# Expert loop of a mixture-of-experts step: moving the two activation transposes from TensorE and ScalarE to VectorE, with weight rows loaded in a matching order

## Chip, core and metric

The kernel runs on one core of a Trainium2 chip. The metric is the device time of one execution in microseconds (us): the median of several runs. The profile is of one further execution.

## What is computed

The reference is one layer of a hybrid decoder (512 prompt tokens behind 16 learned meta tokens, and 8 sample tokens): a mixer (gated linear attention beside sliding-window attention), then a mixture of experts, then a final norm. Only the mixture of experts is touched. Cut to what matters:

```python
logits = x2d @ w_router + b_router              # 520 tokens, 32 experts
top_v, top_e = lax.top_k(logits, 4)
gates = softmax(top_v)
def expert_block(xb, e):                        # rows of one expert
    hh = xb @ w_up[e] + b_up[e]                 # 1024 -> 2048
    gate = minimum(hh[:, :1024], 7.0)
    lin = clip(hh[:, 1024:], -7.0, 7.0)
    a = gate * sigmoid(1.702 * gate) * (lin + 1)
    return a @ w_down[e] + b_down[e]            # 1024 -> 1024
y[token] += gates * expert_block(...)           # for the 4 chosen experts
```

Everything is float32. With the inputs that the reference draws, 2080 token slots fall on 32 experts. In blocks of at most 64 slots the experts 0 to 31 need 2 1 2 1 2 1 1 1 2 1 1 2 2 2 2 2 1 1 1 2 2 1 1 1 2 1 2 1 1 1 2 1 blocks, 46 in all: 14 experts take two blocks, 18 take one.

## The kernel before

The kernel first runs the mixer and the router and builds, on the chip, a table of blocks (which expert, which slots, and whether the block's expert is new). Then comes the expert loop, one pass per block of 64 slots, and at the end the four slot outputs of each token are summed and normalised.

**Weights.** `raw` holds the weights of one expert and no more: 12 units of 1 MiB, 8 of `w_up` (`load_up`, line 473) and 4 of `w_down` (`load_down`, line 561). A unit gives each of 128 partitions 8 KiB: one row of `w_up` (2048 numbers) or two rows of `w_down` (2 x 1024). Up unit j is the rows 128j to 128j+127, down unit j the rows 256j to 256j+255, so each unit is one stretch of memory. SyncE asks for them. It refills a unit as soon as TensorE has used it in this block (`up_used`, `dn_used`), and only if the next block has a new expert. So the weights of a new expert stream in while the last block of the old one is computed, and no earlier.

**Rows.** GpSimd gathers the 64 tokens of a block with an indirect DMA (`gather`, line 443). The 128 partitions of `x_rows` hold 64 slots twice: partitions 0 to 63 the first 512 features of each, partitions 64 to 127 the last 512. The same halves hold the up projection in PSUM (banks 0 and 1), the activations `act_g`, and the output `y_rows`, which GpSimd scatters to memory (`scatter`, line 451). GpSimd waits for a scatter to land before it issues the next gather (line 467).

**Transposes before.** The matmuls need features on partitions. `turn_x` (line 1608) transposes the gathered rows on TensorE in four 128x128 pieces into PSUM bank 3, and `move_xT` (line 780) copies them to `xT` on ScalarE. `turn_a` (line 1614) and `move_aT` (line 784) do the same for the activations through PSUM bank 4 into `aT`.

**Order of the work.** Each engine's order is written out by hand. In loop pass b TensorE does `up(b)` (line 1628), `turn_x(b + 1)`, `down(b - 1)` (line 1647), `turn_a(b)`: the down projection is one block behind, so that the activation function (`clamp`, line 1220, `swiglu`, line 1225, on VectorE and `sigmoid` on ScalarE) runs beside it. `up` makes 32 matmul calls over 8 units, `down` 16 over 4 units; each call is two records in the profile, and the two 64-column halves of the array run side by side. After the first unit of `up(b)` TensorE runs `find(b + 1)` (line 1601), a small product that lists the tokens of the next block. ScalarE does `sigmoid(b)`, `move_xT(b + 1)`, `y_out(b - 1)`, `move_aT(b)`. VectorE does, in this order: `indices(b + 1)`, `select` for the up bias, `find_slots(b + 2)`, `clamp(b)`, `swiglu(b)`, `pick_outputs(b - 1)`, `select` for the down bias. GpSimd does `gather(b + 1)`, `scatter(b - 1)`. SyncE does 8 up loads for block b and 4 down loads for block b - 1.

Of the kernel before, what the change touches and what calls it, by code (L numbers as in the profile page):

```python
# [63 lines left out]
def moe_layer(nc, x_prompt, x_sample, state_gla, cache_k, cache_v, meta, bias_tab, g_mix, w_in, w_a_up, b_a,  # L64
# [12 lines left out]
    with ExitStack() as ctx:  # L77
        def sem(name):
            return ctx.enter_context(nc.semaphore(name))
# [51 lines left out]
        xT = R("xT", [P, 4, P])  # L131
        aT = R("aT", [P, 4, P])
# [168 lines left out]
        xT_psum, xT_ready = sem("xT_psum"), sem("xT_ready")  # L301
# [3 lines left out]
        aT_psum, aT_ready = sem("aT_psum"), sem("aT_ready")  # L305
# [70 lines left out]
        def _(pool):  # L376
# [66 lines left out]
            def gather(b):  # L443
                pool.wait_ge(idx_ready, b + 1)
                if not (isinstance(b, int) and b == 0):
                    pool.wait_ge(xT_psum, b)
                pool.sem_inc(rows_asked, 1)
                pool.indirect_dma_start(x_rows[:], None, xn_halves,  # L448
                                        bass.IndirectOffsetOnAxis(ap=row_idx[:, 0:1], axis=0),
                                        bounds_check=last_row, oob_is_err=False).then_inc(gathered, 16)  # L450
# [21 lines left out]
        def _(sp):  # L472
            def load_up(e, j, cond):
                src = w_up[0, column(e), P * j:P * j + P, :].rearrange("a p n -> p (a n)")
# [86 lines left out]
            def load_down(e, j, cond):  # L561
                src = w_down[0, column(e), 2 * P * j:2 * P * (j + 1), :].rearrange("a (p r) n -> p (a r n)", r=2)
# [47 lines left out]
        def _(act):  # L610
# [169 lines left out]
            def move_xT(b):  # L780
                act.wait_ge(xT_psum, b + 1)
                act.activation(xT[:], ps[:, 3, :].rearrange("p (k q) -> p k q", k=4), ACT.Copy).then_inc(xT_ready, 1)  # L782

            def move_aT(b):
                act.wait_ge(aT_psum, b + 1)
                act.activation(aT[:], ps[:, 4, :].rearrange("p (k q) -> p k q", k=4), ACT.Copy).then_inc(aT_ready, 1)

# [10 lines left out]
            move_xT(0)  # L798
            sigmoid(0)
            move_xT(1)  # L800
            move_aT(0)
            act.wait_ge(table_made, 1)
            nb = block_count(act)
            with act.Fori(1, nb) as b:
                sigmoid(b)
                move_xT(b + 1)
                y_out(b - 1)
                move_aT(b)
# [8 lines left out]
        def _(dve):  # L817
# [412 lines left out]

            find_slots(own, 0)
            indices(own, 0)
            select(sel_up, 0, sel_up_ready)
            find_slots(own, 1)
            indices(own, 1)
# [6 lines left out]
            swiglu(own, 0)  # L1242
            before_loop = own.n
            nb = block_count(dve)
            with dve.Fori(1, nb) as b:
# [7 lines left out]
                swiglu(o, b)  # L1253
                pick_outputs(b - 1)
                dve.wait_ge(dn_bias_done, b)
                select(sel_dn, b, sel_dn_ready)
                assert o.n == STEPS, o.n
# [32 lines left out]
        def _(pe):  # L1290
# [317 lines left out]
            def turn_x(b):  # L1608
                pe.wait_ge(gathered, 16 * b + 16)
                for h in range(4):  # L1610
                    ins = pe.transpose(ps[:, 3, P * h:P * h + P], x_rows[:, P * h:P * h + P], ident[:])  # L1611
                ins.then_inc(xT_psum, 1)

            def turn_a(b):

                pe.wait_ge(a_ready, b + 1)
                for h in range(4):
                    u, r = h // 2, h % 2
                    ins = pe.transpose(ps[:, 4, P * h:P * h + P], act_g[:, 2 * P * u + r:2 * P * (u + 1):2], ident[:])  # L1619
                ins.then_inc(aT_psum, 1)  # L1620

# [6 lines left out]
            def up(b):  # L1628
# [6 lines left out]
                pe.wait_ge(xT_ready, b + 1)  # L1635
                for j in range(UPU):
                    pe.wait_ge(landed[j], 16 * b + 16)
                    for bank in range(2):
                        for i in range(2):
                            c = FF * bank + HF * i  # L1640
                            ins = mm(ps[SUB * i:SUB * i + SUB, bank, :], xT[:, j % 4, SUB * (j // 4):SUB * (j // 4) + SUB],  # L1641
# [5 lines left out]
            def down(b):  # L1647
# [3 lines left out]
                pe.wait_ge(aT_ready, b + 1)  # L1651
                for j in range(DNU):
                    pe.wait_ge(landed[UPU + j], 16 * b + 16)
                    for r in range(2):
                        for i in range(2):
                            ins = mm(ps[SUB * i:SUB * i + SUB, 2, :], aT[:, 2 * (j % 2) + r, SUB * (j // 2):SUB * (j // 2) + SUB],  # L1656
# [6 lines left out]
            turn_x(0)  # L1663
            up(0)
            turn_x(1)
            turn_a(0)
# [50 lines left out]
```

## Time and profile before

| | us |
|---|---|
| Median of 3 runs | 1549.63 (1547.12 to 1549.8) |
| The profiled execution, its own time | 1542.3 |
| Its span, first to last instruction | 1540.5 |
| Expert loop, from the second block's index list to the last down matmul (382.55 to 1489.87) | 1107.3 |

The page gives the engines' busy time over the span: TensorE matmuls 1393.8 us (90%), VectorE 412.1 us (27%), ScalarE 217.8 us (14%), GpSimd 108.2 us (7%). How to read it: the span falls into the mixer and router (to about 347 us), the loop, and the final sum (from about 1490 us), and the loop itself is not even, since a block whose successor has the same expert asks for no weights. The expert loop has to be read by stretches between such blocks, with the memory rate of each beside it.

### The profile page before, as it was taken

Reading aid. Unit: us, or ns where it says so; the run is one execution under the profiler, and the core shown is the slowest. Engines: PE = TensorE matmul, PEld = TensorE weight load, DVE = VectorE, ACT = ScalarE, POOL = GpSimd, SP = SyncE. Lnnn points to the kernel's source line nnn. Section 1 sums busy time; section 2 is a strip of 40 time slices with the busy share of each in tenths; the row PEclk is TensorE's granted clock in tenths of the full one; section 3 lists DMA queues with packets and bytes.
Section 4 is the critical chain, followed back from the end, with each engine's and each line's share of the span. In section 5 each row is a group of like instructions: output and inputs, shape, how many; then the busy total and the mean of one; then the engine's idle time right before and its main releaser. Section 6 shows DMA issues by size and latency. Waiting matters only on the chain.

```text
span 1540.5 us, 21414 instructions
## 1 busy us (share of the span) xinstructions
PE 1393.8 (90%) x6999; PEld 580.4 (38%) x6999; DVE 412.1 (27%) x1011; ACT 217.8 (14%) x419; POOL 108.2 (7%) x151
## 2 busy tenths in 40 slices
PE   8999999966999999899999999998999899998960
PEld 7866556632333333233333333332333233332310
DVE  3433356632211211121112112211111112211118
ACT  4121233310001010000101001000000001000002
POOL 3000000000010000001010010000001010000100
PEclk9989969987999999999999999999999999999985
DMA  9313101253989899999966678999699998999856
GB/s 356 77 47 123 50 16 56 110 204 128 394 340 378 346 398 421 421 402 422 401 253 242 253 330 336 397 422 420 241 413 421 421 398 353 399 422 421 372 202 266
DMA packets 83515, 464.98 MB, mean 302 GB/s; under 512 B 11890, under 2 KB 20708, under 8 KB 33074
## 3 DMA queue, kind: packets, MB, share of 16 engines
q1 hardware_dynamic: 75438, 445.69, 71.8%
q0 software_dynamic: 7440, 17.30, 3.0%
q10 hardware_dynamic: 612, 1.67, 0.3%
q8 instruction: 15, 0.25, 0.1%
q14 instruction: 10, 0.08, 0.0%
HBM read 625.47 MB, written 22.38 MB: 421 GB/s over the span
## 4 chain that ended last, share of the span: by engine, by line
PE 58%; DMA 30%; DVE 4%; issue 4%; ACT 2%; SPq 1%; POOLq 0%; DVEq 0%
PE ps L1656 18%; PE ps L1641 17%; DMA x_rows<-expert_inputs,row_idx 11%; DMA slot_outputs<-y_rows,out_idx 11%; DMA raw<-in_w_down_dram 8%; PE ps L1354 4%; PE ps L1331 4%; PE ps L1553 4%; PE ps L1611 2%; PE ps L1624 2%; DVE t_x L1283 1%; ACT y_rows L795 1%; PE ps L1619 1%; PE ps L1514 1%; PE ps L1513 1%
## 5 line engine op out<-in xcount | busy, mean ns | idle before, releaser
L1641 PE MATMUL ps<-raw,xT 128*64 128x512 f32 x2944 | 656.3, 596 | 14.4 <-DMA raw<-in_w_up_dram 14.4
L1641 PEld LDWEIGHTS ps<-raw,xT 128*64 128x64 f32 x2944 | 205.1, 137 | 399.5 <-issue 355.6
L1656 PE MATMUL ps<-raw,aT 128*64 128x512 f32 x1472 | 328.1, 595 | 8.4 <-DMA raw<-in_w_down_dram 8.1
L1656 PEld LDWEIGHTS ps<-raw,aT 128*64 128x64 f32 x1472 | 102.4, 137 | 203.6 <-issue 178.3
L1222 DVE TENSOR_SCALAR act_g<-ps 128x512 f32<-128x512 f32 x46 | 31.8, 691 | 447.9 <-PE ps L1641 447.9
L790 ACT ACTIVATE act_s<-act_g 128x512 f32<-128x512 f32 x46 | 29.0, 630 | 700.9 <-DVE act_g L1222 700.9
L1207 DVE TENSOR_REDUCE found<-ps 128x2 f32<-128x8 f32 x47 | 7.8, 166 | 411.3 <-PE ps L1604 411.3
L456 POOL DMA_INDIRECT slot_outputs<-y_rows,out_idx x46 | 46.3, 1007 | 750.5 <-ACT y_rows L795 750.5
L795 ACT ACTIVATE y_rows<-ps 128x512 f32<-128x512 f32 x46 | 27.5, 598 | 303.4 <-PE ps L1656 303.4
L448 POOL DMA_INDIRECT x_rows<-expert_inputs,row_idx x47 | 48.6, 1034 | 299.5 <-issue 265.3
L1611 PE MATMUL ps<-ident,x_rows 128*128 128x128 f32 x188 | 31.6, 291 | 37.2 <-DMA x_rows<-expert_inputs,row_idx 37.2
L1354 PE MATMUL ps<-w_c_cols,hT 128*128 128x512 f32 x128 | 59.4, 618 | 0.0
L1553 PE MATMUL ps<-w_out_sb,mixT 128*128 128x512 f32 x128 | 56.7, 597 | 2.5 <-DVE mixT L1056 2.5
L1611 PEld LDWEIGHTS ps<-ident,x_rows 128*128 128x128 f32 x188 | 20.1, 142 | 76.1 <-DMA x_rows<-expert_inputs,row_idx 59.9
L1619 PEld LDWEIGHTS ps<-ident,act_g 128*128 128x128 f32 x184 | 25.4, 207 | 39.0 <-issue 36.5
L1199 DVE TENSOR_TENSOR hit<-slots_row,shifted 128x640 bf16<-128x640 f32 x48 | 39.6, 825 | 1.6
L1331 PE MATMUL ps<-hT,w_a_cols 128*128 128x268 f32 x160 | 36.6, 390 | 0.0
L1619 PE MATMUL ps<-ident,act_g 128*128 128x128 f32 x184 | 34.2, 308 | 2.3 <-DVE act_g L1229 2.3
L1354 PEld LDWEIGHTS ps<-w_c_cols,hT 128*128 128x128 f32 x128 | 24.6, 197 | 29.7 <-issue 29.7
L1553 PEld LDWEIGHTS ps<-w_out_sb,mixT 128*128 128x128 f32 x128 | 23.7, 190 | 30.9 <-issue 30.6
L1331 PEld LDWEIGHTS ps<-hT,w_a_cols 128*128 128x128 f32 x160 | 30.3, 190 | 6.1 <-issue 0.4
L782 ACT ACTIVATE xT<-ps 128x512 f32<-128x512 f32 x47 | 27.6, 588 | 32.8 <-PE ps L1611 32.7
(309 smaller groups left out, 918.6 us busy)
## 6 DMA issues: line engine op xcount, KB each, us to landing
raw<-in_w_up_dram SPq DMA_DIRECT2D x368, 1024.0 KB
raw<-in_w_down_dram SPq DMA_DIRECT2D x184, 1024.0 KB
t_slots<-slot_outputs SPq DMA_DIRECT2D x8, 1024.0 KB, 13.4
w_c_cols<-in_w_in_dram SPq DMA_DIRECT2D x1, 4096.0 KB, 31.2
w_out_sb<-in_w_out_dram SPq DMA_DIRECT2D x1, 4096.0 KB, 14.7
w_a_cols<-in_w_in_dram SPq DMA_DIRECT2D x1, 2624.0 KB, 13.0
x_sb<-in_x_prompt_dram SPq DMA_DIRECT2D x4, 512.0 KB, 5.5
w_b_cols<-in_w_in_dram SPq DMA_DIRECT2D x1, 2048.0 KB, 17.9
```

The lines of the kernel that those rows point to most:

```text
L448: pool.indirect_dma_start(x_rows[:], None, xn_halves, bass.IndirectOffsetOnAxis(ap=row_idx[:, 0:1], axis=0), bounds_check=last_row, oob_is ...
L456: pool.indirect_dma_start(slot_halves, bass.IndirectOffsetOnAxis(ap=out_idx[:, 0:1], axis=0), y_rows[:], None, bounds_check=last_out, oob_ ...
L795: act.activation(y_rows[:], ps[:, 2, :], ACT.Copy).then_inc(y_ready, 1)
L1199: dve.tensor_tensor(hit[:], slots_row[:, 0:SUB].unsqueeze(1).unsqueeze(1).to_broadcast(everywhere), shifted[:].unsqueeze(2).unsqueeze(2).t ...
L1222: dve.tensor_scalar(act_g[:], ps[:, 0, :], LIMIT, None, ALU.min).then_inc(g_ready, 1)
L1331: ins = mm(ps[:, n % 4, 0:HALF], w[:, k, c0:c0 + P], hT[:, k, half], start=(k == 0), stop=(k == KT - 1))
L1354: ins = mm(ps[:, bank, 0:n], hT[:, k, a:z], w[:, k, c0:c0 + n], start=(k == 0), stop=(k == KT - 1))
L1553: ins = mm(ps[0:r, 6 + n, :], mixT[:, k, 0:r], w_out_sb[:, k, 512 * n:512 * n + 512], start=(k == 0), stop=(k == KT - 1))
L1611: ins = pe.transpose(ps[:, 3, P * h:P * h + P], x_rows[:, P * h:P * h + P], ident[:])
L1619: ins = pe.transpose(ps[:, 4, P * h:P * h + P], act_g[:, 2 * P * u + r:2 * P * (u + 1):2], ident[:])
L1641: ins = mm(ps[SUB * i:SUB * i + SUB, bank, :], xT[:, j % 4, SUB * (j // 4):SUB * (j // 4) + SUB], raw[:, SLOT[j], c:c + HF], start=False, ...
L1656: ins = mm(ps[SUB * i:SUB * i + SUB, 2, :], aT[:, 2 * (j % 2) + r, SUB * (j // 2):SUB * (j // 2) + SUB], raw[:, SLOT[UPU + j], D * r + HF ...
```

## The change

The two TensorE transposes, their PSUM banks and the two ScalarE copies are taken out. VectorE transposes from SBUF to SBUF in 32x32 squares: 8 instructions for a block's rows and 8 for its activations, each reading 32 partitions x 256 numbers with a stride and writing 32 partitions x 256 numbers. A square transpose can move a group of 32 features only as a whole, so feature 8p + c now lies on partition p in slice c. The weight rows must stand in the same order: up unit c is now the rows c, 8 + c, 16 + c, ... (8 KiB on each partition as before, 64 KiB apart in memory), down unit c the row pairs 8p + 2c, 8p + 2c + 1 (8 KiB, 32 KiB apart). In VectorE's order `turn_x(b + 1)` comes right after `swiglu(b)`, and `turn_a(b)` last in the pass. `turn_a(b)` waits until `down(b - 1)` has read the old `aT`; `turn_x(b + 1)` waits until `up(b)` is done with `xT` and the gather has landed. `gather(b)` now waits for VectorE's transposes of block b - 1.

```diff
-        xT = R("xT", [P, 4, P])
-        aT = R("aT", [P, 4, P])
+        xT = R("xT", [P, UPU, SUB])
+        aT = R("aT", [P, DNU, 2, SUB])
...
             def gather(b):
                 pool.wait_ge(idx_ready, b + 1)
                 if not (isinstance(b, int) and b == 0):
-                    pool.wait_ge(xT_psum, b)
+                    pool.wait_ge(xT_ready, 8 * b)
...
             def load_up(e, j, cond):
-                src = w_up[0, column(e), P * j:P * j + P, :].rearrange("a p n -> p (a n)")
+                src = w_up[0, column(e)].rearrange("a (p c) n -> c p (a n)", c=UPU)[j]
...
             def load_down(e, j, cond):
-                src = w_down[0, column(e), 2 * P * j:2 * P * (j + 1), :].rearrange("a (p r) n -> p (a r n)", r=2)
+                src = w_down[0, column(e)].rearrange("a (p c r) n -> c p (a r n)", c=DNU, r=2)[j]
...
             with act.Fori(1, nb) as b:
                 sigmoid(b)
-                move_xT(b + 1)
                 y_out(b - 1)
-                move_aT(b)
...
+            def turn(dst, dst_at, src, src_at, done):
+                for side in range(2):
+                    for group in range(2):
+                        rows_in = slice(SUB * side + 32 * group, SUB * side + 32 * group + 32)
+                        for parity in range(2):
+                            rows_out = slice(SUB * side + 32 * parity, SUB * side + 32 * parity + 32)
+                            dve.transpose(dst_at(dst[rows_out], group), src_at(src[rows_in], parity)).then_inc(done, 1)
+            def turn_x(b):
+                if not (isinstance(b, int) and b == 0):
+                    dve.wait_ge(up_used, UPU * b)
+                dve.wait_ge(gathered, 16 * b + 16)
+                turn(xT, lambda t, group: t[:, :, 32 * group:32 * group + 32],
+                     x_rows, lambda t, parity: t.rearrange("p (q r c) -> p q c r", q=2, c=UPU)[:, parity], xT_ready)
+            def turn_a(b):
+                dve.wait_ge(a_ready, b + 1)
+                dve.wait_ge(dn_used, DNU * b + 2 * DNU)
+                turn(aT, lambda t, group: t[:, :, :, 32 * group:32 * group + 32],
+                     act_g, lambda t, parity: t.rearrange("p (q r c t) -> p q c t r", q=2, c=DNU, t=2)[:, parity], aT_ready)
...
                 clamp(b)
                 swiglu(o, b)
+                turn_x(b + 1)
                 pick_outputs(b - 1)
                 dve.wait_ge(dn_bias_done, b)
                 select(sel_dn, b, sel_dn_ready)
+                turn_a(b)
...
                 bias(1, FF, sel_up).then_inc(up_bias_done, 1)
-                pe.wait_ge(xT_ready, b + 1)
+                pe.wait_ge(xT_ready, 8 * b + 8)
...
             with pe.Fori(1, nb) as b:
                 up(b)
-                turn_x(b + 1)
                 down(b - 1)
-                turn_a(b)
```

The slices of `xT` and `aT` that `up` and `down` read change to match. Ahead of the loop `turn_x(0)` stands after `find_slots(1)`, and `turn_x(1)` and `turn_a(0)` after `swiglu(0)`.

## Rows read from the trace of the kernel before

**Rows 1.** The page: memory rate in 40 equal slices of the span.

```profile
GB/s 356 77 47 123 50 16 56 110 204 128 394 340 378 346 398 421 421 402 422 401 253 242 253 330 336 397 422 420 241 413 421 421 398 353 399 422 421 372 202 266
```

**Rows 2.** Timeline of one pass without a wait (start us, us, engine, line, tile).

```profile
926.18 0.14 PEld L1641 LDWEIGHTS ps<-raw,xT 128*64 128x64 f32 x2 [0.28 <-issue]
927.14 0.66 PE L1611 MATMUL ps<-ident,x_rows 128*128 128x128 f32 x4
...
927.73 0.41 PE L1624 MATMUL ps<-bias_parts,sel_dn 128*64 128x512 bf16 x2
...
927.97 7.03 PE L1656 MATMUL ps<-raw,aT 128*64 128x512 f32 x32
...
934.93 0.74 PE L1619 MATMUL ps<-ident,act_g 128*128 128x128 f32 x4
...
935.60 0.62 PE L1624 MATMUL ps<-bias_parts,sel_up 128*64 128x512 bf16 x4
...
938.08 12.24 PE L1641 MATMUL ps<-raw,xT 128*64 128x512 f32 x56
```

**Rows 3.** The same timeline and its next pass: VectorE, GpSimd, and TensorE behind a gather.

```profile
927.26 0.69 DVE L1222 TENSOR_SCALAR act_g<-ps 128x512 f32<-128x512 f32 x1 [9.40 <-PE ps L1641]
...
927.86 0.68 DVE L1223 TENSOR_SCALAR act_l<-ps 128x512 f32<-128x512 f32 x1
...
929.31 0.69 DVE L1229 TENSOR_TENSOR act_g<-act_l,act_s 128x512 f32<-128x512 f32 x1
...
944.37 1.02 POOL L448 DMA_INDIRECT x_rows<-expert_inputs,row_idx  x1 [6.87 <-issue]
...
951.51 0.66 PE L1611 MATMUL ps<-ident,x_rows 128*128 128x128 f32 x4 [1.19 <-DMA x_rows<-expert_inputs,row_idx]
```

**Rows 4.** Waits between 382.55 and 1489.87 us (total us, times, longest).

```profile
PE ps L1611 <- DMA x_rows<-expert_inputs,row_idx: 28.1, 23, 2.1
...
PE ps L1641 <- DMA raw<-in_w_up_dram: 14.4, 21, 1.3
```

**Rows 5.** Windows cut at starts of L1207: length, busy time (PE, PEld, DVE, ACT, POOL), PEclk, DMA share, GB/s.

```profile
382.55:451.89 69.34, 69.34 (x347) 24.21 (x345) 14.18 (x40) 6.93 (x12) 6.09 (x6) 1.00 0.87 353
451.89:524.99 73.10, 71.05 (x347) 24.59 (x345) 14.27 (x39) 7.04 (x12) 6.44 (x6) 0.98 0.88 360
524.99:652.13 127.14, 117.55 (x577) 39.69 (x575) 23.73 (x65) 11.88 (x20) 10.15 (x10) 1.00 1.01 413
652.13:748.29 96.16, 92.67 (x462) 32.28 (x460) 18.91 (x53) 9.57 (x16) 8.12 (x8) 1.00 0.99 406
748.29:938.29 190.00, 185.19 (x922) 64.56 (x920) 37.89 (x105) 18.93 (x32) 16.29 (x16) 1.00 0.69 281
...
1064.40:1111.51 47.11, 46.29 (x232) 16.14 (x230) 9.46 (x26) 4.73 (x8) 4.06 (x4) 1.00 0.69 273
...
1237.54:1307.97 70.43, 69.42 (x347) 24.22 (x345) 14.20 (x40) 7.04 (x12) 6.09 (x6) 1.00 0.91 371
1307.97:1434.28 126.31, 117.54 (x577) 39.68 (x575) 23.63 (x65) 11.89 (x20) 10.15 (x10) 1.00 1.00 414
1434.28:1489.87 55.59, 51.84 (x247) 17.14 (x243) 9.61 (x27) 4.73 (x8) 4.06 (x4) 1.00 0.67 268
```

**Rows 6.** Groups by line, 400 to 1450 us: a short VectorE instruction (busy us, mean ns).

```profile
L1217 DVE TENSOR_TENSOR sel_up<-expert_of_row,blk_expert 128x64 bf16<-128x64 f32 x43 | 9.7, 225 | 5.3
```

**Rows 7.** Timeline of the loop's start: first rows landed, first block's end.

```profile
357.71 1.11 PE L1611 MATMUL ps<-ident,x_rows 128*128 128x128 f32 x4 [9.04 <-DMA x_rows<-expert_inputs,row_idx]
...
359.61 3.62 PE L1641 MATMUL ps<-raw,xT 128*64 128x512 f32 x8
...
377.94 0.69 DVE L1229 TENSOR_TENSOR act_g<-act_l,act_s 128x512 f32<-128x512 f32 x1
...
380.29 1.91 PE L1641 MATMUL ps<-raw,xT 128*64 128x512 f32 x8
```

**Rows 8.** Window 1506 to 1518 us, while `t_slots` loads 8 KiB pieces 16 KiB apart (columns as rows 5).

```profile
1506.00:1518.00 12.00, 0.00 (x0) 0.00 (x0) 10.65 (x10) 4.17 (x7) 0.00 (x0) 0.50 1.01 427
```

More of the change, by code:

```diff
@@ L300, in moe_layer @@
         out_idx_ready, y_free = sem("out_idx_ready"), sem("y_free")
-        xT_psum, xT_ready = sem("xT_psum"), sem("xT_ready")
+        xT_ready = sem("xT_ready")
         sel_up_ready, sel_dn_ready, up_bias_done, dn_bias_done = (
@@ L304, in moe_layer @@
         g_ready, up_read, sigm_ready, a_ready = sem("g_ready"), sem("up_read"), sem("sigm_ready"), sem("a_ready")
-        aT_psum, aT_ready = sem("aT_psum"), sem("aT_ready")
+        aT_ready = sem("aT_ready")
         y_ready, scattered = sem("y_ready"), sem("scattered")
@@ L778, in _ @@
             act.wait_ge(mixer_left, 4)
[L780 to L786, printed above, removed]
             def sigmoid(b):
@@ L797, in _ @@
             act.sem_inc(y_ready, 1)
-            move_xT(0)
             sigmoid(0)
-            move_xT(1)
-            move_aT(0)
             act.wait_ge(table_made, 1)
@@ L1234, in _ @@
             find_slots(own, 1)
+            turn_x(0)
             indices(own, 1)
@@ L1242, in _ @@
             swiglu(own, 0)
+            turn_x(1)
+            turn_a(0)
             before_loop = own.n
@@ L1606, in find @@
                 ins.then_inc(list_psum, 1)
[L1608 to L1620, printed above, removed]
             def bias(bank, c0, sel):
@@ L1640, in up @@
                             c = FF * bank + HF * i
-                            ins = mm(ps[SUB * i:SUB * i + SUB, bank, :], xT[:, j % 4, SUB * (j // 4):SUB * (j // 4) + SUB],
+                            ins = mm(ps[SUB * i:SUB * i + SUB, bank, :], xT[:, j, :],
                                      raw[:, SLOT[j], c:c + HF], start=False, stop=(j == UPU - 1))
@@ L1650, in down @@
                 bias(2, 2 * FF, sel_dn).then_inc(dn_bias_done, 1)
-                pe.wait_ge(aT_ready, b + 1)
+                pe.wait_ge(aT_ready, 8 * b + 8)
                 for j in range(DNU):
@@ L1655, in down @@
                         for i in range(2):
-                            ins = mm(ps[SUB * i:SUB * i + SUB, 2, :], aT[:, 2 * (j % 2) + r, SUB * (j // 2):SUB * (j // 2) + SUB],
+                            ins = mm(ps[SUB * i:SUB * i + SUB, 2, :], aT[:, j, r, :],
                                      raw[:, SLOT[UPU + j], D * r + HF * i:D * r + HF * i + HF], start=False,
@@ L1662, in _ @@
             find(0)
-            turn_x(0)
             up(0)
-            turn_x(1)
-            turn_a(0)
             pe.wait_ge(table_made, 1)
```

## Prediction

> **What bounds the kernel now.** I read the page first: its row of memory rates [rows 1] sits at 421 to 422 GB/s in some slices of the loop and at 241 to 253 in others. So one share of busy time cannot answer; the loop has to be cut where the need for weights changes. A block whose successor has the same expert asks for nothing; all others ask for 12 MiB. I therefore cut the loop at the start of the last block of each two-block expert, and took a window for each stretch up to the next such cut [rows 5]. Counting the experts between cuts by the list of blocks, there are four kinds: **pairs** (2 blocks, 1 weight load; five of them, four standing together in the window of 190.00 us), **triples** (3 blocks, 2 loads; three), one **quad** (4 blocks, 3 loads), and **quintets** (5 blocks, 4 loads; four, of which the first and the last are shown, 127.14 and 126.31). A tail of 55.59 us holds the last two blocks, and the first block stands ahead of the first cut.
>
> Pairs run at 273 to 281 GB/s: memory has room, TensorE decides. Quintets run at 413 to 414 GB/s with a DMA share of 1.00, and 5 blocks take 126.3 us, 25.3 each: memory decides. Next I read TensorE's side in one pass without waits [rows 2]: transposes at 927.14, down bias, down, transposes at 934.93, up bias, up with the small list product inside, and the next transposes at 950.25 would close a pass of 23.1 us. Three such passes are 69.3, exactly the first triple [rows 5]. The rest of a pair is one wait: GpSimd may gather only when its last scatter has landed, so the rows come about 1.2 us after TensorE wants them [rows 3], 28.1 us over 23 passes [rows 4].
>
> **TensorE's part of the change.** `turn_x` occupies 927.14 to 927.73, 0.59 us; `turn_a` 934.93 to 935.60, 0.67 us [rows 2]. Both go: 1.26 us a pass, so a pass is 23.11 - 1.26 = 21.85 us. Bounds: the gap in weight loads around a transposing step, 926.18 to 927.73 = 1.55 us against 0.43 us for the usual pair of loads, would give 1.12 us, and likewise behind `down`, together some 2.3 us a pass; on the low side, if each boundary kept 0.2 us of draining, 0.9 us. I take 1.26 because matmul starts, not weight loads, are what the pass is made of. Half of 28.1 us would be the gather waits in stretches bound by TensorE; they go too, for the following reason.
>
> **VectorE's part.** No transpose of its kind is in the trace. Nearest rows: a 512-element float32 instruction lasts 0.69 us and the next starts 0.60 us after it [rows 3]; a 64-element one lasts 225 ns [rows 6]. Along that line 256 elements last 0.425 us and follow each other every 0.345 us, whatever the number of partitions. Eight of them: 8 x 0.345 + 0.08 = 2.84 us per turn, two turns a pass, 5.7 us on an engine that is busy 9.46 us in 47.1 [rows 5]. Bounds: 8 x 0.225 = 1.8 us (all of it fixed cost) and 8 x 0.69 = 5.5 us (each number costs twice). The Trainium skill, "VectorE: DVE Perf Modes", section on the TRN2 errata, warns that small tiles pay SBUF latency per instruction, its measured fixed term being about 150 cycles; as an estimate from that page 256 elements without overlap are 0.42 us, a turn 3.4 us, and the sum below would lose about 1 us. No run here shows it for a transpose.
>
> **Does a turn hide?** `turn_x(b + 1)` starts when `swiglu(b)` ends, 929.31 + 0.69 = 930.00, which is 2.8 us after `up` ended [rows 3]. TensorE needs `xT` after the down bias, `down` (0.24 + 6.96 us) and the up bias (0.46): 7.66 us after `up` ended. So a turn may take 7.66 - 2.8 = 4.8 us; 2.84 leaves 2 us. The gather that was 1.2 us late (2.1 at most [rows 4]) still lands before 2.8 us, even with `down` starting sooner by the 0.67 us that `turn_a` took, so VectorE does not wait for it either: that is why the 28.1 us end. `turn_a(b)` begins when `down(b - 1)` ends and has all of `up(b + 1)`, 14.5 us, before `down(b)`. Queued behind it on VectorE is only `indices(b + 2)`, which finds its list 2.5 us after `down` ended and so starts 0.4 us late; the gather behind it waits longer than that for the scatter (6.87 us at 944.37, [rows 3]), so this costs nothing. ScalarE loses two copies that nobody will miss; `y_out` has its queue to itself. The cycle through GpSimd, down end to scatter to gather to turn, is 951.51 - 935.00 = 16.5 us plus 2.84, below 21.85.
>
> **Memory's part.** The 12 units are the same bytes in the same 8 KiB pieces; only their distance in memory changes, from touching to 64 KiB and 32 KiB. I cost this at nothing, after the nearest row: `t_slots` reads 8 KiB pieces 16 KiB apart at 427 GB/s [rows 8]. The bound on the other side is open, and is the first rival.
>
> **The sum.** A stretch lasts as long as the longer of TensorE's passes and memory's bytes. Bytes of a quintet: 127.14 us x 413 GB/s = 52.5 MB, of which 4 loads are 50.3, the gathers and scatters the rest; 52.5 MB at 421 are 124.7 us, and the row shows 2.4 more, latency at its ends.
> - Pairs: from 190.00 + 47.11 = 237.1 to 5 x 2 x 21.85 = 218.5: **-18.6**.
> - Triples: 69.34 + 73.10 + 70.43 = 212.9. After: TensorE 65.55; memory 26.3 MB (73.10 x 360) / 421 + 2.4 = 64.9. So 3 x 65.55 = 196.7: **-16.2**.
> - Quad: 96.16 before. Memory: 96.16 x 406 = 39.0 MB / 421 + 2.4 = 95.1, TensorE only 4 x 21.85 = 87.4: **-1.0**.
> - Quintets: memory's before and after: **0**. What TensorE saves here it waits for weights instead. 20 of 46 blocks are in this place.
> - Tail (55.59 us): its first pass, 23.1 us and a gather wait of 1.2, cannot go under one load's up units (8 x 1.05 MB / 421 = 19.9, plus 2.4, 22.3); the last down units are asked for during `down` of the block before and come late as now: **-2.0**.
> - Start: the first rows land at 357.7 and TensorE multiplies at 359.61 [rows 7]; with VectorE at 357.7 + 2.84 = 360.5, +0.9. Block 1: `swiglu(0)` ends at 378.63, plus 2.84 = 381.5, against 380.29 [rows 7]: +1.2. Together **+2.1**.
>
> Sum: -18.6 - 16.2 - 1.0 - 2.0 + 2.1 = -35.7 us, 2.3%. The profiled execution would go from 1542.3 (span 1540.5) to 1506.6; it lay 7.3 us below the median of the runs, 1549.63, and I set the forecast against that: **1514 us**.
>
> **Rivals.**
> *Memory slows down (ends slower).* The 64 KiB pitch makes the streams of 16 engines meet in the same part of memory, and the rate falls. For: the quintets are bound by memory already, and every load goes through the new pitch. Against: the 16 KiB pitch ran at 427. Price: the 25 loads of quintets, quad and triples (16 + 3 + 6) take 12.58 MB / 421 = 29.9 us each, 747 us, so 5% less rate costs 39 us and cancels the gain; that is the deciding point, about 400 GB/s. At 380 GB/s it is 80 us lost, 1514 + 80 = 1594; pairs would hold until about 310. The Trainium skill, "DMA: Bandwidth & Descriptors", section "Latency and other measured facts", tells of copies that ran at half rate with row pitches of large powers of two, still full at 512 KiB and worse from 2 MiB; by it 64 KiB would be safe. No row here has that pitch. Chance 7%, at some 1560 to 1600.
> *The squares are slow on VectorE.* At 0.69 us each (5.5 us a turn) TensorE waits 5.5 - 4.8 = 0.7 us a pass in 19 passes of pairs and triples, 13 us back: 1527, still faster. From about 0.8 us each, 6.4 a turn, the 1.6 us a pass eat the gain; at 7 us a turn, 2.2 us a pass make pairs 48.1 us (+0.7 each), triples 72.2 (+1.2 each) and the start 10 us later, some 15 us in all: 1565. For: strided reads, 32 of 128 lanes, four-byte squares. Against: nothing in the trace prices elements above 1.07 ns. Chance of a middling 1520 to 1540, 9%; of slower than before, 5%.
> *Memory was the bound everywhere that counts.* If the cuts mislead and triples are also held by loads (73.10 for one hints at it), only pairs gain: -18.6 - 2 + 2 = 1531. Chance 8%.
> *More than forecast.* If a pass falls to 20.8 (the 2.3 us of the weight loads), pairs give 10 us more, triples are stopped by memory at 64.9, 2 more: 1502. Chance 7%.
>
> **How the numbers follow.** A measurement of this kernel can tell about 0.2%, 3.1 us, from no change. Forecast 60%, its own range 1506 to 1522. Range for 8 in 10: from 1502 (the upper gain) to 1540 (slow squares, or memory 3 to 4% slower). Faster 0.84: forecast 60, more 7, pairs only 8, middling squares 9; within 0.2%: 0.04 (the deciding point of either rival hit by chance); slower 0.12 (memory 7, squares 5).
>
> **What would show it.** In the profile after: VectorE's 16 transposes a pass at 0.35 to 0.45 us each; no matmul group on an identity in the loop; the gather wait gone from TensorE; pairs at 43.7 us; quintets unchanged near 126 with TensorE's wait for up weights well above the 14.4 us of now [rows 4]; slices at 421 GB/s staying at 421. Quintets above 128 us with a rate under 415 would prove the memory rival; waits of `up` on VectorE's `xT` would prove slow squares; both would make the forecast wrong.

## The result, and the profile after

The changed kernel took 1519.87 us (median of 4 runs, 1519.27 to 1523.29) against 1549.72 us for the kernel before: ratio 0.9824, interval 0.98 to 0.9848. The forecast was 1514, the range 1502 to 1540. The profiled execution has a span of 1517.6 us against 1540.5, 22.9 us less (the profiled execution of before lay below its median, so the medians differ by more, 29.9 us).

The page of the changed kernel, its rate row and its two new groups:

```profile
span 1517.6 us, 21459 instructions
...
GB/s 359 81 24 148 51 16 43 78 255 119 259 357 412 364 422 420 421 422 421 415 273 271 285 346 337 420 422 421 277 411 421 420 413 360 423 420 421 358 200 268
...
L1225 DVE STREAM_TRANSPOSE aT<-act_g 32x256 f32<-32x256 f32 x368 | 233.2, 634 | 27.1 <-PE ps L1658 17.0
L1225 DVE STREAM_TRANSPOSE xT<-x_rows 32x256 f32<-32x256 f32 x376 | 237.8, 633 | 16.3 <-DMA x_rows<-expert_inputs,row_idx 6.0
```

An instruction that I had at 0.425 us takes 0.634, and there are 744 of them. The rate still stands at 420 to 423 GB/s where it stood at 421 to 422 [rows 1]. One pass in a pair, from the timeline:

```profile
913.54 0.39 PE L1626 MATMUL ps<-bias_parts,sel_dn 128*64 128x512 bf16 x2
913.75 7.04 PE L1658 MATMUL ps<-raw,aT 128*64 128x512 f32 x32
...
915.80 0.69 DVE L1216 TENSOR_TENSOR act_g<-act_l,act_s 128x512 f32<-128x512 f32 x1
...
916.42 5.28 DVE L1225 STREAM_TRANSPOSE xT<-x_rows 32x256 f32<-32x256 f32 x8
920.62 0.60 PE L1626 MATMUL ps<-bias_parts,sel_up 128*64 128x512 bf16 x4
...
921.83 1.94 PE L1643 MATMUL ps<-raw,xT 128*64 128x512 f32 x8 [0.61 <-DVE xT L1225]
921.93 5.29 DVE L1225 STREAM_TRANSPOSE aT<-act_g 32x256 f32<-32x256 f32 x8
...
923.91 12.24 PE L1643 MATMUL ps<-raw,xT 128*64 128x512 f32 x56
```

Against [rows 2, 3]: the boundaries where `turn_x` and `turn_a` stood are gone, VectorE's turn starts where it was forecast, 2.9 us after `up`, but it lasts 5.3 us, and TensorE waits for it with its first up matmul. A pass is 22.44 us, not 21.85. The same cuts as in [rows 5], the last stretch again up to the end of the last down matmul:

```profile
392.05:461.38 69.33, 67.49 (x333) 22.38 (x331) 44.38 (x88) 3.68 (x6) 6.10 (x6) 1.00 0.92 367
461.38:528.71 67.33, 65.49 (x323) 21.82 (x321) 44.38 (x88) 3.68 (x6) 6.10 (x6) 1.00 0.96 390
528.71:653.33 124.62, 112.28 (x537) 34.87 (x535) 74.11 (x145) 6.14 (x10) 10.18 (x10) 1.00 1.01 422
653.33:747.49 94.16, 88.64 (x432) 28.54 (x430) 59.25 (x117) 4.91 (x8) 8.14 (x8) 1.00 1.01 419
747.49:927.25 179.76, 174.90 (x860) 58.28 (x858) 118.30 (x232) 9.83 (x16) 17.36 (x16) 1.00 0.74 295
...
1050.93:1096.08 45.15, 43.93 (x218) 14.66 (x216) 29.58 (x59) 2.46 (x4) 4.07 (x4) 1.00 0.74 300
...
1221.17:1288.74 67.57, 65.74 (x325) 21.92 (x323) 44.36 (x87) 3.69 (x6) 6.11 (x6) 1.00 0.95 384
1288.74:1413.13 124.39, 112.27 (x537) 34.86 (x535) 74.09 (x145) 6.14 (x10) 10.18 (x10) 1.00 1.01 421
1413.13:1467.52 54.39, 47.64 (x219) 15.35 (x215) 29.66 (x59) 2.46 (x4) 4.07 (x4) 0.94 0.63 255
```

| term (us of the profiled span) | forecast | measured, cut at the index lists | the same, cut at the first up matmul |
|---|---|---|---|
| five pairs | -18.6 | 224.9 - 237.1 = -12.2 | -12.8 |
| three triples | -16.2 | 204.2 - 212.9 = -8.7 | -9.2 |
| quad | -1.0 | -2.0 | -2.0 |
| four quintets | 0 | 497.8 - 505.6 = -7.8 | -6.6 |
| tail, to the last down matmul | -2.0 | 54.4 - 55.6 = -1.2 | 59.5 - 57.8 = +1.7 |
| start | +2.1 | +9.5 | +6.6 |
| behind the last down matmul | 0 | -0.5 | -0.6 |
| sum | -35.7 | -22.9 | -22.9 |

The last column is there because the cut itself moved. In the changed kernel the index list stands on VectorE behind `turn_a`: it starts 5.4 us after the block's first up matmul (927.25 against 921.83), where before it was 2.2 us (938.29 against 936.06). Cut at the lists, about 3 us of the tail are booked on the start. Where TensorE decides, the last column is the one to read.

The waits between 383 and 1470 us say the same from TensorE's side. Of [rows 4] the gather wait is gone, the wait for up weights has grown from 14.4 to 24.9, and two new ones stand there:

```profile
PE ps L1643 <- DVE xT L1225: 27.4, 36, 6.0
PE ps L1643 <- DMA raw<-in_w_up_dram: 24.9, 38, 1.2
PE ps L1658 <- DMA raw<-in_w_down_dram: 19.5, 36, 1.0
...
PE ps L1658 <- DVE aT L1225: 4.8, 1, 4.8
```

The start, again from the timeline:

```profile
380.88 0.69 DVE L1216 TENSOR_TENSOR act_g<-act_l,act_s 128x512 f32<-128x512 f32 x1
381.49 5.22 DVE L1225 STREAM_TRANSPOSE xT<-x_rows 32x256 f32<-32x256 f32 x8
...
386.84 3.68 PE L1643 MATMUL ps<-raw,xT 128*64 128x512 f32 x8 [5.95 <-DVE xT L1225]
```

Here nothing hides `turn_x(1)`: no `down` is running yet. TensorE stands idle for 5.95 us, and the group of 8 that took 1.91 us before [rows 7] takes 3.68 behind it: the granted clock is 0.72 on average from 380 to 392 us, a mix of 2.4 and 1.2 GHz. `up(1)` begins 6.55 us later than before (386.84 against 380.29), 4.4 over the forecast: two turns at 5.3 in place of 2.84, less 0.6 us by which the first rows landed earlier (357.15 against 357.71). The other 3 us to the second index list (392.05 against 382.55) are the slow group, 1.8 us, and 1.2 us in which the list waits on VectorE for `turn_a(0)`.

### The profile page after: what moved, and what is told of

Read it like the earlier page. It is cut to its first block, busy times and chain, and to the rows that moved or that the text cites. A ratio compares the mean times of both kernels' runs of the same rounds, so it can differ in the third digit from the quotient of the medians.

```text
span 1517.6 us, 21459 instructions
## 1 busy us (share of the span) xinstructions
PE 1341.1 (88%) x6627; PEld 539.7 (36%) x6627; DVE 880.3 (58%) x1755; ACT 164.9 (11%) x326; POOL 110.9 (7%) x151
## 4 chain that ended last, share of the span: by engine, by line
PE 57%; DVE 17%; DMA 14%; issue 7%; SPq 4%; ACT 1%; DVEq 0%; POOLq 0%
PE ps L1643 36%; DMA raw<-in_w_down_dram 9%; DVE xT L1225 8%; PE ps L1370 4%; PE ps L1347 4%; PE ps L1569 4%; DMA raw<-in_w_up_dram 3%; SPq L479 2%; SPq L567 2%; DVE t_x L1299 2%; PE ps L1658 2%; DVE act_l L1214 2%; DVE act_g L1209 2%; DVE act_l L1210 1%; DMA w_a_cols<-in_w_in_dram 1%
## 5 line engine op out<-in xcount | busy, mean ns | idle before, releaser
L1643 PE MATMUL ps<-raw,xT 128*64 128x512 f32 x2944 | 663.3, 599 | 64.9 <-DVE xT L1225 39.4
L1643 PEld LDWEIGHTS ps<-raw,xT 128*64 128x64 f32 x2944 | 201.6, 137 | 466.9 <-issue 391.6
L1658 PE MATMUL ps<-raw,aT 128*64 128x512 f32 x1472 | 332.2, 598 | 24.3 <-DMA raw<-in_w_down_dram 19.5
L1225 DVE STREAM_TRANSPOSE aT<-act_g 32x256 f32<-32x256 f32 x368 | 233.2, 634 | 27.1 <-PE ps L1658 17.0
L1225 DVE STREAM_TRANSPOSE xT<-x_rows 32x256 f32<-32x256 f32 x376 | 237.8, 633 | 16.3 <-DMA x_rows<-expert_inputs,row_idx 6.0
L1370 PEld LDWEIGHTS ps<-w_c_cols,hT 128*128 128x128 f32 x128 | 24.9, 200 | 30.0 <-issue 30.0
L1214 DVE SCALAR_TENSOR_TENSOR act_l<-act_l,act_g 128x512 f32<-128x512 f32 x46 | 31.8, 692 | 1.6
L1216 DVE TENSOR_TENSOR act_g<-act_l,act_s 128x512 f32<-128x512 f32 x46 | 31.8, 692 | 1.6
L1210 DVE TENSOR_SCALAR act_l<-ps 128x512 f32<-128x512 f32 x46 | 31.3, 681 | 0.0
L1299 DVE SCALAR_TENSOR_TENSOR t_x<-t_slots,gates,t_x 128x1024 f32<-128x1024 f32 (+1 forms) x20 | 25.6, 1281 | 8.2 <-DMA t_slots<-slot_outputs 7.4
## 6 DMA issues: line engine op xcount, KB each, us to landing
w_b_cols<-in_w_in_dram SPq DMA_DIRECT2D x1, 2048.0 KB, 18.7
```

The lines of the kernel that those rows point to most:

```text
L1210: dve.tensor_scalar(act_l[:], ps[:, 1, :], LIMIT, -LIMIT, ALU.min, ALU.max).then_inc(up_read, 1)
L1214: o.do(dve.scalar_tensor_tensor(act_l[:], act_l[:], 1.0, act_g[:], ALU.add, ALU.mult))
L1225: dve.transpose(dst_at(dst[rows_out], group), src_at(src[rows_in], parity)).then_inc(done, 1)
L1299: do(dve.scalar_tensor_tensor(x2[0:r, :], y4[0:r, k, :], gates[0:r, t, k:k + 1], x2[0:r, :], ALU.mult, ALU.add))
L1370: ins = mm(ps[:, bank, 0:n], hT[:, k, a:z], w[:, k, c0:c0 + n], start=(k == 0), stop=(k == KT - 1))
L1643: ins = mm(ps[SUB * i:SUB * i + SUB, bank, :], xT[:, j, :], raw[:, SLOT[j], c:c + HF], start=False, stop=(j == UPU - 1))
```

## Experiments

Ratios are to the kernel before on the same chip, with a 95% interval; stretches are from the profiled execution ("pairs" is a quarter of the window with four pairs).

**1. Whose gain or loss is the order of the weight rows?** `e1_rows_only` is the kernel before with

```diff
-                src = w_up[0, column(e), P * j:P * j + P, :].rearrange("a p n -> p (a n)")
+                src = w_up[0, column(e)].rearrange("a (p c) n -> c p (a n)", c=UPU)[j]
-                src = w_down[0, column(e), 2 * P * j:2 * P * (j + 1), :].rearrange("a (p r) n -> p (a r n)", r=2)
+                src = w_down[0, column(e)].rearrange("a (p c r) n -> c p (a r n)", c=DNU, r=2)[j]
```

and `e2_squares_only` the changed kernel with these lines undone.

> The kernel before with the new order of weight rows alone (64 and 32 KiB pitch); the transposes stay on TensorE in the old order, so products pair other rows with other features and the output is another one, the work is the same. Theory (memory does not care about the pitch): nothing moves, 1549 us within 3, quintets 126 us at 413 to 419 GB/s, pairs 47.3. Rival (the new order is what made the quintets of the changed kernel 1.9 us shorter): quintets 124.4, time about 1541. Rival (the pitch costs rate and hides a larger gain): quintets above 128, time above 1556.

> The changed kernel with the old order of weight rows; the output is another one, the work is the same. Theory: as the changed kernel, 1520 us within 3, quintets 124.4, pairs 44.9. Rival (the new order sped memory up): quintets 126, time about 1528. Rival (the new order slows memory): below 1514.

Measured: e1 1553.07 us, ratio 1.0047 (1.003 to 1.0065); pairs 48.5, the four quintets 509.5 in sum (before 505.6). e2 1518.68 us, ratio 0.9841 (0.9811 to 0.987); pairs 45.0, the quintets 495.9 (changed kernel 497.8). The changed kernel itself, run again as e5, had 0.9836. The rate between 600 and 650 us was 421 or 422 GB/s in all four kernels. So the order of the rows does not shorten the quintets: they are short in e2 and long in e1, that is, short where TensorE does not turn the gathered rows (in e11 below, where it still turns the activations, they are 500.6). Nor does it cost the changed kernel anything that these intervals can show. Alone it makes the kernel before slower by 0.3 to 0.65%, which I had not expected. In e1 TensorE's wait for gathered rows is longer than in [rows 4]:

```profile
PE ps L1611 <- DMA x_rows<-expert_inputs,row_idx: 33.0, 23, 2.5
```

and three passes take 26.8 to 27.4 us, where before had one. What such a pass is, the kernel before shows in its first long triple (73.10 us), in timeline and window:

```profile
465.97 0.88 PE L1611 MATMUL ps<-ident,x_rows 128*128 128x128 f32 x4 [2.05 <-DMA x_rows<-expert_inputs,row_idx]
...
467.21 8.27 PE L1656 MATMUL ps<-raw,aT 128*64 128x512 f32 x32
```

```profile
464.00:472.00 8.00, 6.03 (x24) 2.23 (x26) 2.93 (x6) 1.23 (x2) 0.00 (x0) 0.79 1.02 425
```

A gather wait of 2.05 us was followed by a granted clock of 0.79 and a `down` of 8.27 us where 7.03 is usual; behind the other 22 gather waits, of up to 1.89 us, `down` took 7.03 at a clock of 1.00. In e1 three waits (2.50, 1.94 and 1.95 us) were followed by a `down` of 8.4 to 8.7 us. The 4.9 us of longer waits and some 3.3 us more of slow `down` are about what e1 lost; why the new order delays the gather is open.

**2. What does a turn cost the whole?** `e3_two_wide` keeps all and makes the squares cheap. Each square stays in its own 32 partitions, so `xT` and `aT` hold other numbers.

```diff
-                            dve.transpose(dst_at(dst[rows_out], group), src_at(src[rows_in], parity)).then_inc(done, 1)
...
+                for group in range(2):
+                    dve.transpose(dst_at(dst[:], group), src_at(src[:], group)).then_inc(done, 1)
```

> The changed kernel, each turn done by 2 instructions of 128 partitions x 256 numbers in place of 8 of 32 x 256; the squares stay in their own group of 32 partitions, so the operands hold other numbers, and all else is kept. Theory (an instruction costs 0.66 us by its numbers per partition, whatever the partitions): a turn takes 1.35 us, TensorE no longer waits for xT, pairs 43.7 and triples 65.6, block 1 about 4 us earlier, in all 17 to 20 us below the changed kernel, near 1502 us. Rival (cost goes with the count of squares, 64 a turn): a turn stays at 5.3 us and the time at 1520.

Measured: 1492.2 us, ratio 0.9662 (0.9635 to 0.9689). The group and the two windows:

```profile
L1221 DVE STREAM_TRANSPOSE xT<-x_rows 128x256 f32<-128x256 f32 x94 | 54.5, 618 | 7.3 <-DMA x_rows<-expert_inputs,row_idx 7.2
```

```profile
734.66:907.55 172.89, 172.89 (x858) 58.70 (x856) 55.59 (x136) 9.83 (x16) 16.29 (x17) 1.00 0.76 305
907.55:1032.84 125.29, 112.61 (x537) 34.81 (x535) 34.84 (x86) 6.14 (x10) 10.19 (x11) 1.00 1.01 419
```

128 partitions cost what 32 cost: 0.618 us. With turns out of the way a pass is 172.89 / 8 = 21.61 us, and index list to index list of block 1 takes 19.8 us, not 25.7. The quintet stays at 125: memory. So slow squares cost the changed kernel about 1.7% in ratio and 23.8 us between the two profiled spans, more than the 17 to 20 expected: pairs and triples give 18 us and the start and the tail some 10, while the quintets are 4 us longer than in the changed kernel. And 21.61 is what TensorE's part of the change gives when undisturbed: 1.50 us a pass where I had 1.26.

**3. Is it the count of numbers, or how they are read?** `e6_half_squares` cuts every transposing instruction in two; `e7_dense_read` lets `turn_x` read neighbours (`"p (q c r) -> p q c r"` for `"p (q r c) -> p q c r"`), so that features and weight rows no longer match, and leaves `turn_a` as it is.

```diff
-                            dve.transpose(dst_at(dst[rows_out], group), src_at(src[rows_in], parity)).then_inc(done, 1)
+                            d, s = dst_at(dst[rows_out], group), src_at(src[rows_in], parity)
+                            n = d.shape[1] // 2
+                            for part in range(2):
+                                ins = dve.transpose(d[:, n * part:n * part + n], s[:, n * part:n * part + n])
+                            ins.then_inc(done, 1)
```

> The changed kernel with each transposing instruction cut in two: 16 of 32 partitions x 128 numbers a turn, the same result. Theory (an instruction follows the last after 0.127 us of fixed cost and two cycles of 0.96 GHz for each number, 0.66 us at 256): 16 x (0.127 + 0.267) = 6.3 us a turn, TensorE waits 1.5 us a pass, pairs about 46.9. Rival (nearly all of the 0.66 us goes by numbers): 5.3 us a turn, as before. Rival (0.4 us fixed, one cycle a number, as the prediction had it but with more overhead): 16 x 0.53 = 8.5 us a turn, pairs above 50.

> The changed kernel, where turn_x reads runs of 32 neighbouring numbers in place of every eighth one, turn_a as it was; features then sit in another order than the weight rows, so the output is another one. Theory (the cost goes by the count of numbers): xT instructions 0.63 us like those of aT. Rival (the stride of 32 bytes on the read side halves the speed): xT instructions near 0.42 us and a turn_x of 3 us, TensorE's wait for xT gone, pairs 43.7, aT still 0.63 us.

Measured, e6 first, then e7:

```profile
L1228 DVE STREAM_TRANSPOSE xT<-x_rows 32x128 f32<-32x128 f32 x752 | 260.0, 379 | 16.2 <-DMA x_rows<-expert_inputs,row_idx 5.9
```

```profile
L1225 DVE STREAM_TRANSPOSE aT<-act_g 32x256 f32<-32x256 f32 x368 | 233.3, 634 | 53.7 <-PE ps L1658 43.5
L1225 DVE STREAM_TRANSPOSE xT<-x_rows 32x256 f32<-32x256 f32 x376 | 163.5, 435 | 16.7 <-DMA x_rows<-expert_inputs,row_idx 6.3
```

and one turn of e7 in the timeline:

```profile
905.04 3.70 DVE L1225 STREAM_TRANSPOSE xT<-x_rows 32x256 f32<-32x256 f32 x8
```

In e6 a turn of 16 took 5.8 us where 6.3 was expected (one run, 1533.0 us, pairs 45.9): from 128 to 256 numbers the duration grows by 255 ns, 2.0 ns a number. My theory of two cycles for each number, whatever the reading, fell with e7: read without a stride, the same 256 numbers take 0.435 us, almost the 0.425 of the forecast, beside `aT` at 0.634 in the same run. The squares are not slow; a read step of 8 numbers, 32 bytes, makes them slow. (The Trainium skill, "SBUF — State Buffer", section "Door 1", has the rule: lines of 16 bytes, full speed only with at least two accesses to a line, so four float32 as the longest free step. The trace agrees as far as it goes, with 0.634 us at a step of 8 and 0.435 at a step of 1; no run here has a step of 4.) The eight follow each other every 0.46 us, not 0.345: there is no overlap between them. In e6 there is some: its instructions of 0.379 us start by turns 0.33 and 0.39 us after each other, 0.33 between the two halves of one former instruction, which write the same 32 partitions, and 0.39 where the next one writes others. That the change of partitions takes the overlap away fits this, but no run tests it by itself. At 3.7 us a turn is hidden, pairs are 43.2 again, and e7 took 1502.44 us in its one run.

**4. Can VectorE's order hide the slow turn?** `e4_turn_before_swiglu`:

```diff
                 clamp(b)
-                swiglu(o, b)
                 turn_x(b + 1)
+                swiglu(o, b)
```

> The changed kernel with turn_x(b + 1) moved ahead of swiglu(b) on VectorE, right behind clamp(b). Theory (TensorE waits 0.6 us a pass because the turn ends 8.1 us after up where 7.66 are to be had): the turn now ends 6.7 us after up, the wait goes, pairs 43.7, triples 65.6, block 1 1.4 us earlier, about 12 us below the changed kernel, 1508 us. Rival (the gather lands too late for the earlier turn, or the later swiglu and turn_a push the index list and the next gather back by more than the scatter hides): the wait stays or grows, 1520 or more.

`e8_reordered` moves more:

```diff
                 select(sel_up, b + 1, sel_up_ready)
+                turn_a(b - 1)
                 find_slots(o, b + 2)
                 clamp(b)
+                pick_outputs(b - 1)
+                turn_x(b + 1)
                 swiglu(o, b)
-                turn_x(b + 1)
-                pick_outputs(b - 1)
...
-                turn_a(b)
```

> The changed kernel with VectorE's order rewritten, same result: pick_outputs and turn_x(b + 1) between clamp(b) and swiglu(b), and turn_a(b) moved behind the index list and the up bias selection of the next pass. Theory (a late turn_x costs TensorE 0.6 us a pass, and a turn_a ahead of the index list delays the gather that the earlier turn_x then waits for): TensorE waits for xT nearly nowhere, pairs 43.2 to 43.7, triples 65 to 65.6, some 14 us below the changed kernel, ratio to before about 0.974. Rival (the gather is held by the scatter alone): as with turn_x moved alone, 0.978.

> The changed kernel itself once more, so that the runs beside it have it on the same chip. Theory and rival alike: ratio to the kernel before 0.982 to 0.984.

Measured: e4 1511.2 us, ratio 0.9784 (0.9757 to 0.9812); e8 1508.17 us, 0.9751 (0.9705 to 0.9797); e5 1519.67 us, 0.9836 (0.9788 to 0.9884). Waits in e4 and then in e8, 395 to 1470 us:

```profile
DVE xT L1225 <- DMA x_rows<-expert_inputs,row_idx: 32.9, 27, 1.9
...
PE ps L1643 <- DVE xT L1225: 14.1, 20, 1.1
```

```profile
DVE xT L1225 <- DMA x_rows<-expert_inputs,row_idx: 20.4, 23, 2.1
...
PE ps L1643 <- DVE xT L1225: 5.7, 9, 1.4
```

TensorE's wait fell from 21.4 us (the 27.4 above without the 6.0 at the start, which this window leaves out) to 14.1 and 5.7, but not to nothing: the earlier turn now meets the late gather, which was hidden behind `swiglu`. Pairs came to 44.0 in both. In e4 TensorE's wait at the start fell from 5.95 to 4.50 us, but the second list came no sooner (26.3 us after the first), against my expectation, because `turn_a(0)` now begins later and holds back the index list. e8 is the fastest kernel here that computes the whole result. Its interval against the kernel before just overlaps that of e5, but the two ran on one chip, and there its four runs took 1504.87 to 1509.2 us and those of e5 1518.4 to 1523.91: about 11 us apart, clear of the spread.

**5. Is each half of the change worth having?** `e11_x_only` keeps the rows on VectorE and gives the activations back to TensorE and ScalarE (the removed `turn_a`, `move_aT` and down rows return).

```diff
...
             with pe.Fori(1, nb) as b:
                 up(b)
                 down(b - 1)
+                turn_a(b)
```

> Half of the change, same result: the gathered rows turned by VectorE with the new order of up rows, the activations turned by TensorE and copied by ScalarE as before, down rows as before. Theory (a pass is TensorE's work or the end of turn_x, whichever is later): pass 21.6 + 0.7 = 22.3 us, turn_x just hidden behind it, pairs 44.7 against 45.1 of the full change, the tail 3 us shorter since the last activations need no squares: 3 to 5 us below the full change, so its activation half brings nothing. Rival (both halves carry their share): 10 us above the full change, ratio 0.989 or more.

Measured: 1516.53 us, ratio 0.981 (0.9793 to 0.9827). The four pairs:

```profile
748.90:928.52 179.62, 179.62 (x890) 61.85 (x888) 78.49 (x168) 14.60 (x24) 16.25 (x16) 1.00 0.72 294
```

179.62 us against 179.76 with both halves. TensorE is now busy all the time, since its transposes of the activations fill the gap in which it would wait for `xT`. With turns of 5.3 us the activation half brought nothing; the gain is the rows' half. In the tail it even costs: from the first up matmul of the last block but one to the last down matmul e11 takes 54.2 us, e3 with its cheap turns 53.6, the changed kernel 59.5 and the kernel before 57.8.

**6. Squares without a stride, and the weights to match.** `e9_dense` orders features in runs; `e10_dense_first` adds a buffer for block 0's `xT`, so that `turn_x(1)` can run beside `up(0)`.

```diff
-                src = w_up[0, column(e)].rearrange("a (p c) n -> c p (a n)", c=UPU)[j]
+                src = w_up[0, column(e)].rearrange("a (g c r) n -> c g r (a n)", g=4, c=UPU)[j]
-                src = w_down[0, column(e)].rearrange("a (p c r) n -> c p (a r n)", c=DNU, r=2)[j]
+                src = w_down[0, column(e)].rearrange("a (g c r t) n -> c g r (a t n)", g=4, c=DNU, t=2)[j]
...
```

> The changed kernel with another feature order, same result: feature 256g + 32c + r on partition 32g + r of up slice c, features 256g + 64c + 2r and the next one on that partition of down slice c. turn_x reads runs of 32 neighbours, turn_a every second number; a weight unit is 4 runs of 32 rows. Theory (the read stride of 8 numbers is what makes a square slow): turn_x takes 3.7 us, TensorE never waits for it, pairs 43.2, some 17 us below the changed kernel, ratio to before 0.971 to 0.974; for turn_a at stride 2 either 0.43 or 0.63 us an instruction, which changes only the tail. Rival (the new pieces of memory cost rate): quintets above 127.

> As e9_dense, and xT of block 0 gets a buffer of its own, so that turn_x(1) runs while up(0) still multiplies. Theory (block 1 pays for TensorE's idle time while swiglu(0) and turn_x(1) run, and for the half clock that follows it): from the first index list to the second 19 to 20 us in place of 24, no 3.68 us group at the head of up(1), 4 us below e9_dense. Rival (the clock falls anyway): 1 to 2 us at most.

Measured: e9 4306.21 us, ratio 2.7852 (2.7798 to 2.7905), e10 4303.71 us, 2.7847. Both squares were quick in e9, `turn_a` with its step of 2 numbers too, but memory collapsed:

```profile
L1225 DVE STREAM_TRANSPOSE aT<-act_g 32x256 f32<-32x256 f32 x368 | 160.5, 436 | 859.0 <-PE ps L1658 848.9
```

```profile
1000.00:1200.00 200.00, 80.87 (x214) 18.95 (x214) 23.41 (x58) 2.45 (x4) 4.06 (x4) 0.62 0.26 109
```

A DMA share of 0.26 and 109 GB/s, a quarter of 421: the source now begins with a dimension of 4, and the share is that of 4 engines in 16. (The Trainium skill, "DMA: Bandwidth & Descriptors", section on why a DMA increments its semaphore by 16, has the rule: the number of engines is the largest up to 16 that divides the slowest dimension of both sides. The share of 0.26 agrees.) The buffer of e10 did shorten the start, from 22.7 us between the first two index lists in e9 to 19.1, as expected; the 2.5 us between the two medians are too few to tell beside 4300. `e12_two_halves` goes around that with two loads a unit, each contiguous and with 64 partitions in front:

```diff
+                for side in range(2):
+                    at = HF * side + SUB * j
+                    src = w_up[0, column(e), at:at + SUB, :].rearrange("a p n -> p (a n)")
+                    dst = raw[SUB * side:SUB * side + SUB, SLOT[j], :]
...
```

> Same result as the changed kernel, reads of the squares as in e9_dense and the buffer of e10_dense_first, but a weight unit is now two loads of 64 partitions, each one stretch of memory: rows 64c to 64c + 63 and 512 + 64c to 512 + 64c + 63 for up unit c, 128 rows each for down unit c. Theory (e9_dense fell to 108 GB/s because its source began with a dimension of 4 and so used a quarter of the DMA engines; the squares were right): memory back at 421 GB/s in the quintets and 125 us for each, turns 3.7 us, pairs 43.2, first index list to second 20 us, ratio to before 0.967 to 0.971, the fastest of all runs with the right result. Rival (SyncE's 24 issues a pass in place of 12 come late): quintets above 128, ratio above 0.98.

Measured: 2238.46 us, ratio 1.4472 (1.4406 to 1.4538), a window of the loop:

```profile
1300.00:1500.00 200.00, 133.37 (x478) 34.01 (x474) 50.55 (x123) 6.14 (x10) 8.12 (x8) 0.79 1.02 227
```

This time all engines are busy (1.02), at 227 GB/s: a load into 64 partitions runs at about half the rate of one into 128. My expectation fell, and so did the cause that its rival gave, since the engines were never idle for want of issues. (The Trainium skill, "SBUF — State Buffer", has in "Door 1" that partitions 0 to 63, like 64 to 127, reach only 8 of the 16 ports. Its section "Can I just issue two DMAs to hit both halves?" says that two DMAs at once, one at partition 0 and one at partition 64, gained only 6% over a single one. The 227 GB/s against 421 agree.) The loads of e12 are also half as large as the others, 512 KiB, and no run here separates the two. One thing e12 shows before its weights run late, the start with the extra buffer:

```profile
373.24 3.71 DVE L1234 STREAM_TRANSPOSE xT<-x_rows 32x256 f32<-32x256 f32 x8 [1.45 <-DMA x_rows<-expert_inputs,row_idx]
383.35 1.91 PE L1652 MATMUL ps<-raw,xT 128*64 128x512 f32 x8
...
388.00 0.17 DVE L1203 TENSOR_REDUCE found<-ps 128x2 f32<-128x8 f32 x1
```

`turn_x(1)` runs beside `up(0)`, the first group of `up(1)` takes 1.91 us, and the second index list comes 18.7 us after the first, where the changed kernel needs 25.7 and e7, with the same turn of 3.7 us, 24.0. So the idle time and the half clock behind it made the start dear. No kernel here has dense reads, one 128-partition load a unit and this start together; whether one can be had stays open.

## Why the prediction was right, and where its terms were off

The forecast's mechanism held, and its median came within 6 us, in part by luck. The sum was a gain of 35.7 us of the profiled span, and the profiled span gained 22.9: by the last column of the table pairs, triples and the start fell short by 17 us together and the tail by 4, while the quintets, which had been put at nothing, gave 7 back. Another 7 us came from the baseline: the forecast was set against the median of before, 7.3 us above its profiled execution, while the profiled execution of the changed kernel lay at its median. Beside the experiments the kernel before had medians of 1543.0 to 1545.8 us, and there the same change was worth 26 us (e5, 1519.67 against 1545.8).

- **TensorE's part.** Right, and mis-sized: 1.26 us a pass, measured 23.11 - 21.61 = 1.50 (e3, e7). The matmul starts leave out that the next matmul also starts a tenth of a microsecond sooner behind `up` and `down` when it is not a transposing one (12.07 in place of 12.17 us after the start of the last 56 of `up`, 6.87 in place of 6.96 after that of `down`).
- **VectorE's part.** This is the step that failed: "256 elements last 0.425 us and follow each other every 0.345 us", 2.84 us a turn. A turn takes 5.29. The sum had two things wrong. The overlap: even dense reads follow each other every 0.46 us, 3.70 a turn (e7), 0.86 more than forecast, but still hidden. And the duration: the line through the rows prices numbers read one after another, `turn` reads every eighth, and that adds the other 1.59 us, which no longer hide. The upper bound, 5.5, held, and with it the rival of the slow squares, in its middling form, though it put the time at 1527.
- **Does a turn hide?** The limit of 4.8 us was about right: 5.29 exceeds it by 0.5, the timeline shows TensorE idle for 0.61 us, and the pass is 22.44 us. Against the 21.61 of e3 that is 0.83: the first up matmul, which there starts 0.43 us after the up bias, starts 1.21 after it, more than the idle time shows, since the two would overlap. Against the forecast it is 0.59 in 19 passes of pairs and triples, 11 of the 14 us by which these fell short; the first triple's first pass, 24.44 us, holds 2 more. The index list, said to start 0.4 us late behind `turn_a`, starts some 3 us late, and this too costs nothing: the gather comes 7.8 us after the scatter in both kernels.
- **The gather wait** ended, as argued: the row is gone from TensorE, and VectorE waits for rows once.
- **Memory's part.** Free, as costed, in the changed kernel (the intervals of e2 and e5 overlap). The rival of a slower memory did not come, save for the 0.3 to 0.65% that the order costs the kernel before.
- **Quintets.** I had 0 and they gave 7.8 (6.6 by the other cut). The "2.4 us more, latency at its ends" was no latency: 124.62 x 422 = 52.6 MB is what passed before, now at 422 GB/s in place of 413. The missing time was one gap in the stream of loads inside the stretch, 24 to 36 us behind its start. Before, then changed:

```profile
549.00:561.00 12.00, 12.00 (x61) 3.98 (x59) 1.86 (x7) 0.00 (x0) 1.31 (x2) 1.00 0.92 340
```

```profile
552.71:564.71 12.00, 12.00 (x60) 4.02 (x58) 5.57 (x10) 0.63 (x1) 1.03 (x1) 1.00 1.02 422
```

12 us at 340 in place of 421 GB/s are 2.3 us. TensorE is busy throughout, so it was memory that lacked work. That TensorE released the units too late, and that a shorter pass without the gather wait closes the gap, fits the order of the loads but is argued, not shown. How much is gained depends on more than the length of the pass: with 21.61 us a pass e3 has quintets of 501.6 in sum, longer than the 497.8 here.
- **Start.** +9.5 in place of +2.1 by the lists, +6.6 by the first up matmul: two turns of 5.3 us in the open, and behind them a half clock that the sum did not have. **Tail**: the -1.2 that stands beside the forecast -2.0 comes from the moved cut. From the first up matmul of the last block but one to the last down matmul the tail grew by 1.7 us. The last `turn_a` is in the open (4.8 us of wait), which the forecast had left out; without it e11 and e3 have tails 5 to 6 us shorter than the changed kernel.

## What to carry to other kernels

Price a transpose on VectorE by how far apart its inputs lie: with float32, a step of 8 took 1.46 times as long as a step of 1 or 2. A layout that suits the squares must also suit the loads: 128 partitions in one transfer, and a first dimension that all DMA engines can share, were worth far more here than the squares (0.2 us an instruction against a factor of 1.4 to 2.8 on the kernel). A wait of TensorE costs more than its length once the clock falls behind it. And a stretch that is cut at an engine's marker moves with that engine's queue: cut where the engine that decides starts its work.

## What the hardware showed that I had not expected

- A transposing instruction of 128 x 256 numbers takes 0.618 us, one of 32 x 256 0.634: four times the work at the same price, if the layout allows the squares to stay in their partitions.
- A load into 64 partitions moved 227 GB/s with all DMA engines busy, one with a leading dimension of 4 moved 109 GB/s at a share of 0.26, the 128-partition form 421.
- After waits of 2.05 us (before) and 5.95 us (changed) TensorE ran partly at 1.2 GHz: a `down` of 8.27 us for 7.03, a group of 3.68 us for 1.91. After 22 other waits of up to 1.89 us in the kernel before it did not.
